# Delta rule with both directions in one tile's halves, its state steps between inversion levels

## The reference

```python
def chunk_gated_delta_rule(q, k, v, beta, g, s0):      # chunks of C = 64
    G = jnp.cumsum(g, axis=-1)
    decay = jnp.exp(jnp.where(incl, G[..., :, None] - G[..., None, :], -jnp.inf))
    kb = k * beta[..., None]
    a = jnp.where(strict, jnp.einsum('nbhid,nbhjd->nbhij', kb, k) * decay, 0.0)
    m = a + jnp.eye(C, dtype=a.dtype)
    rhs = jnp.concatenate([kb * jnp.exp(G)[..., None], v * beta[..., None]], axis=-1)
    sol = lax.linalg.triangular_solve(m, rhs, left_side=True, lower=True, unit_diagonal=True)
    w, u = sol[..., :dk], sol[..., dk:]
    ...
    def step(s, xs):                                   # the state step, one chunk after another
        v_new = u_c - jnp.einsum('bhcd,bhde->bhce', w_c, s)
        o = jnp.einsum('bhcd,bhde->bhce', qd_c, s) + jnp.einsum('bhij,bhje->bhie', qk_c, v_new)
        s = s * cd_c[..., None, None] + jnp.einsum('bhcd,bhce->bhde', kt_c, v_new)
        return s, o
```

## Time and profile before

| | |
|---|---|
| median of 3 runs | 1901.72 us (1900.16 to 1902.12) |
| profiled execution, its own time | 1902.44 us |
| its span on the core | 1900.6 us |
| PE busy, share of span | 1583.7 us, 83% |
| DVE / ACT / POOL busy | 670.8 / 445.5 / 203.8 us |
| mean granted TensorE clock | 0.925 of full speed |
| HBM traffic | 303.79 MB read, 24.78 MB written |

### The profile page before, as it was taken

The page is one execution under the profiler, slowest core; times in us unless marked ns, Lnnn a source line. Parts: engine busy times, 40 slices in busy tenths (PEclk is TensorE's granted clock), DMA queues, the critical chain, the costliest instruction groups (busy, mean ns, idle before and its releaser), DMA issues.

```text
span 1900.6 us, 36972 instructions
## 1 busy us (share of the span) xinstructions
PE 1583.7 (83%) x16252; PEld 1046.0 (55%) x16252; DVE 670.8 (35%) x1293; ACT 445.5 (23%) x722; POOL 203.8 (11%) x202
## 2 busy tenths in 40 slices
PE   5999956779749999978999877687766976999993
PEld 2554424445437776654655455576765545777662
DVE  5134575552350000013142398544454143000003
ACT  4111284441121111103010256421211032111110
POOL 0000000000001111100000000344441000111103
PEclk8999996998869999989999898899988987999996
DMA  9822461454229999982212000000001414999994
GB/s 347 284 89 89 165 244 43 153 204 179 87 76 341 375 388 389 381 279 74 89 44 92 0 1 1 2 2 2 2 2 67 167 58 163 377 372 388 382 392 155
DMA packets 90218, 330.01 MB, mean 174 GB/s; under 512 B 10612, under 2 KB 16360, under 8 KB 81928
## 3 DMA queue, kind: packets, MB, share of 16 engines
q1 hardware_dynamic: 75920, 287.29, 39.6%
q0 software_dynamic: 9168, 32.65, 6.2%
q10 hardware_dynamic: 5032, 8.65, 1.3%
HBM read 303.79 MB, written 24.78 MB: 173 GB/s over the span
## 4 chain that ended last, share of the span: by engine, by line
PE 69%; DVE 15%; DMA 5%; issue 5%; ACT 4%; ACTq 0%; DVEq 0%; POOL 0%; SPq 0%
PE pairs L191 25%; PE pairs L1241 13%; PE pairs L1253 11%; DMA ring<-in_exp_w 3%; PE pairs L1224 2%; DVE sm L1576 1%; PE pairs L417 1%; PE pairs L1871 1%; PE pairs L957 1%; PE pairs L1642 1%; PE pairs L1873 1%; ACT arena L1511 1%; PE pairs L1078 1%; PE pairs L567 1%; DMA ring<-in_w_in_ab 1%
## 5 line engine op out<-in xcount | busy, mean ns | idle before, releaser
L191 PE MATMUL pairs<-hT,ring 128*128 128x128 f32 (+1 forms) x1120 | 305.6, 435 | 2.1 <-ACT hT L315 2.1
L191 PEld LDWEIGHTS pairs<-hT,ring 128*128 128x128 f32 x1120 | 170.0, 192 | 138.5 <-issue 137.1
L315 ACT ACTIVATE arena<-pairs 128x256 f32<-128x256 f32 (+7 forms) x188 | 120.5, 655 | 517.0 <-PE pairs L191 254.4
L191 PE MATMUL pairs<-ring,hT 128*128 128x512 f32 (+1 forms) x448 | 177.4, 557 | 0.0
L1241 PEld LDWEIGHTS pairs<-arena 128*64 128x64 f32 x4096 | 145.6, 139 | 13.8 <-issue 13.7
L1241 PEld LDWEIGHTS pairs<-arena,ring 128*64 128x64 f32 x4096 | 142.8, 137 | 14.1 <-issue 14.1
L1241 PE MATMUL pairs<-arena 128*64 128x80 f32 x4096 | 148.5, 235 | 2.0 <-ACT arena L1274 1.0
L1241 PE MATMUL pairs<-arena,ring 128*64 128x80 f32 x4096 | 145.6, 233 | 1.1 <-issue 1.1
L191 PEld LDWEIGHTS pairs<-ring,hT 128*128 128x128 f32 x448 | 84.8, 190 | 92.2 <-issue 89.1
L1307 DVE TENSOR_SCALAR hT<-pairs,arena 80x512 f32<-80x512 f32 x32 | 23.9, 747 | 273.1 <-ACT hT L1283 273.1
L1253 PE MATMUL pairs<-ring,arena 128*80 128x512 f32 x256 | 112.8, 593 | 1.1 <-DMA ring<-in_exp_w 1.1
(11 more groups left out here) (374 smaller groups left out, 2168.3 us busy)
## 6 DMA issues: line engine op xcount, KB each, us to landing
arena<-in_exp_w SPq DMA_DIRECT2D x48, 2048.0 KB, 19.4
ring<-in_exp_w SPq DMA_DIRECT2D x48, 2048.0 KB, 21.5
ring<-in_w_mod SPq DMA_DIRECT2D x24, 2048.0 KB, 8.1
ring<-in_w_in_ab SPq DMA_DIRECT2D x5, 2048.0 KB, 11.5
ring<-in_w_in_cd SPq DMA_DIRECT2D x5, 2048.0 KB, 7.8
ring<-in_w_out SPq DMA_DIRECT2D x4, 2048.0 KB, 8.6
moe_rows<-arena POOLq DMA_DIRECT2D x2, 2560.0 KB, 16.2
h_rows<-arena POOLq DMA_DIRECT2D x2, 2560.0 KB, 8.4
```

The lines of the kernel that those rows point to most:

```text
L191: last = pe.matmul(out, lhs(k), rhs(k), start=(k == 0), stop=(k == KD - 1))
L315: return eng.activation(dst, src, ACT.Copy) if eng is nc.scalar else eng.tensor_copy(dst, src)
```

## The change

**Mixed tiles.** A tile m < 4 now holds forward tokens on partitions 0 to 63 (the first half of token tile m) and backward tokens on partitions 64 to 127 (the second half of token tile 3 - m). A step j = 0 to 7 does chunk j of the forward and chunk 7 - j of the backward direction, both in tile `tile_at(j)`; j = 8, 9 are the prompt. Each tile serves two steps. The transposes of k and q and the products `kk` are made once per tile (5 times, 10 before), and `kk` is kept in SBUF by ACT (`kk_read`); DVE's `kk_gated` reads that copy. Two steps (j, j + 1) are inverted together.

**Placing.** The state steps of j - 2 and j - 1 stand between the levels 1 and 3 of the inversions of j and j + 1 on every engine; `state_a` is vs and q times state, `state_b` the other two products. The steps 8 and 9 come at the end. PSUM is used in 8 single banks. `wu` no longer uses block-diagonal operands (no memsets of them).

**Around it.** `conv_pe` turns a tile's halves by two matmuls against the identity; the gates are copied in halves (`read_gate`), the decays' columns rearranged by 28 small copies on DVE (`decay_dve`), constants loaded by 6 more DMAs on SP, and `cyT` puts the halves back by its identity's columns.

```diff
@@ -1690,48 +1715,91 @@
+        tile_at = lambda j: 4 if j >= 8 else j // 2 if j % 2 == 0 else 3 - j // 2
+        half_of = lambda j, d: d ^ (j % 2)
+        first_visit = lambda j: j < 4 or j == 8
+        STATE_STEPS = (0, 1, 2, 3, 4, 5, 6, 9)
+        KX_STEPS = (0, 1, 2, 3, 4, 5, 6, 8, 9)
+        TILE_ORDER = (0, 3, 1, 2, 4)
...
@@ -1739,9 +1807,14 @@ def conv_pe(pe):
-                for t in range(NT):
-                    o = t * P if t < ST else UP0
-                    last = pe.transpose(ps[:, t * P:t * P + P], c[:, o:o + P], ident)
+                for m in range(NT):
+                    out = ps[:, m * P:m * P + P]
+                    if m < ST:
+                        for h, r in enumerate(HALF):
+                            o = P * (m if h == 0 else 3 - m) + CK * h
+                            last = pe.matmul(out[r], c[:, o:o + CK], ident, start=True, stop=True)
+                    else:
+                        last = pe.transpose(out, c[:, UP0:UP0 + P], ident)
...
@@ delta_pe
+            for m in TILE_ORDER[:2]:
+                kq(m)
+                kk(m)
+            for j in range(2):
+                am(j)
+            for i in range(5):
+                j = 2 * i
                 for s in range(1, 6):
+                    for e in range(2):
+                        level_w(j + e, s)
+                    if s in (1, 3) and i == 0:
+                        kq(TILE_ORDER[2 + s // 2])
+                    elif s in (1, 3):
+                        state_a(j - 2 + s // 2)
+                    elif s in (2, 4) and i < 4:
+                        dec(j + 1 + s // 2)
+                    elif s == 5 and i == 2:
+                        kq(ST)
+                    for e in range(2):
+                        level_x(j + e, s)
+                    if s in (1, 3) and i == 0:
+                        kk(TILE_ORDER[2 + s // 2])
+                    elif s in (1, 3):
+                        state_b(j - 2 + s // 2)
+                    elif s in (2, 4):
+                        qd(j - 1 + s // 2)
+                    elif s == 5 and i == 2:
+                        kk(ST)
+                if i < 4:
+                    for e in range(2):
+                        am(j + 2 + e)
+                for e in range(2):
+                    wu(j + e)
+            state_b(8)
+            state_a(9)
+            state_b(9)
...
@@ delta_dve
+            def kk_gated(j):
+                v.wait_ge(S("dl_exp"), j + 1)
+                b_emptied(v, ("kk", tile_at(j)))
+                step(v.tensor_tensor(decays(j), kk_all(tile_at(j)), decays(j), ALU.mult))
...
+                for s in range(1, 6):
+                    if s in (1, 3) and i:
+                        values_new(j - 2 + s // 2)
+                    elif s in (2, 4) and i < 4:
+                        dec_read(v, step, j + 1 + s // 2)
+                    for e in range(2):
+                        x_next(j + e, s)
+                    if s in (1, 3):
+                        if i:
+                            state_new(j - 2 + s // 2)
+                        if i < 4:
+                            diag(v, j + 2 + s // 2)
+                    elif s in (4, 5) and i < 4:
+                        kk_gated(j + s - 2)
+                    if i >= 3:
+                        k = 2 * (i - 3)
+                        if s == 1 and i == 4:
+                            o_sum(v, 7, dscr3, 0)
+                        elif s == 2 and i == 4:
+                            o_scale(1)
+                        elif s == 3:
+                            o_sum(v, 6 + k, dscr3, 0)
+                        elif s == 4:
+                            o_scale(k)
...
@@ delta_act
+            def uw_read(j):
+                if j >= 2:
+                    b_filled(act, ("o", 7) if j == 9 else ("st", j - 2, half_of(j, 1)))
+                for b in range(2):
+                    u = ("wu", j, b)
+                    b_release(copy(act, uw(j)[:, 512 * b:512 * b + 512], b_filled(act, u)), u)
...
+                    if s in (3, 5) and i < 4:
+                        decay_exp(act, j + 2 + s // 5)
...
```

More of the change, by code:

```diff
@@ L42, with __init__ @@
 LAM_INIT = 0.2
-WHOLE = ("ident", "ones", "lo_one", "up_one", "block")
-BLOCKS = ["ident", "lo_neg", "up_neg"] + [f"{d}{s}" for d in "fb" for s in range(6)]
+WHOLE = ("ident", "ones", "cum0", "cum1", "block")
+BLOCKS = ["ident", "neg0", "neg1"] + [f"level{e}{s}" for e in range(2) for s in range(6)]
 class Units:
-    def __init__(self):
-        self.uses = [0] * 4
+    def __init__(self, n=4):
+        self.uses = [0] * n
         self.of = {}
@@ new lines, in build, with b_take, b_finish, b_filled @@
+        bank_free = [S(f"bank_free{i}") for i in range(8)]
+        bank_of = lambda b: PSUM[:, b // 2, 512 * (b % 2):512 * (b % 2) + 512]
+        def b_take(pe, name, b):
+            b, n = banks.add(name, b)
+            if n > 1:
+                pe.wait_ge(bank_free[b], n - 1)
+            return bank_of(b)
+        def b_finish(ins, name):
+            ins.then_inc(bank_full[banks.of[name][0]], 1)
+        def b_filled(eng, name):
+            b, n = banks.of[name]
+            eng.wait_ge(bank_full[b], n)
+            return bank_of(b)
@@ new lines, in dec, with qd, am @@
+            def dec(j):
+                pe.wait_ge(S("dl_diag"), j + 1)
+                u = ("dec", j)
+                b_finish(dec_sums(pe, b_take(pe, u, 6), j), u)
+            def qd(j):
+                pe.wait_ge(S("dl_qd"), j + 1)
+                u = ("qd", j)
+                ps = b_take(pe, u, 7)
+                for h in range(4):
+                    last = pe.transpose(ps[:, h * P:h * P + P], qe(j)[:, h, :], ident)
+                b_finish(last, u)
+            def am(j):
+                pe.wait_ge(S(f"dl_am{j % 2}"), 6 * (j // 2) + 1)
+                u = ("am", j)
+                ps = b_take(pe, u, j % 2)
+                for h in range(4):
+                    for r in HALF:
+                        last = pe.matmul(ps[r, CK * h:CK * h + CK], am64(j)[r, h, :], C64["ident"][r, :],
+                                         start=True, stop=True)
+                b_finish(last, u)
@@ L1930, in delta_pe @@
+            state_b(8)
+            state_a(9)
+            state_b(9)
             pe.wait_ge(S("o_done"), 10)
+            for b in range(8):
+                pe.wait_ge(bank_free[b], banks.uses[b])
             for b in range(4):
@@ L1933, in delta_pe @@
                 ps = take(pe, u)
-                for t in range(NT):
-                    last = pe.transpose(ps[:, t * P:t * P + P], oacc[:, t, b * P:b * P + P], ident)
+                for m in range(NT):
+                    out = ps[:, m * P:m * P + P]
+                    if m < ST:
+                        o, gap = ((0, 448), (128, 192), (192, 64), (64, 320))[m]
+                        out = ps[:, o:o + 2 * gap].rearrange("p (a x) -> p a x", a=2)[:, :, 0:CK]
+                    last = pe.transpose(out, oacc[:, m, b * P:b * P + P], swap if m in (2, 3) else ident)
                 finish(last, u)
@@ L1939, in build, with decay_exp @@
         heads5 = lambda x: x.rearrange("p (t h) d -> p t h d", h=4)
[L1941 to L1944 removed]
+        def decay_exp(act, j):
+            (emptied if j < 2 else b_emptied)(act, ("dec", j))
+            act.activation(decays(j), decays(j), ACT.Exp).then_inc(S("dl_exp"), 1)
         def decay_act(act):
@@ L2049, in delta_dve @@
                 conv_read(v, ct)
+            for c in range(2):
+                step(v.tensor_copy(swap[:, CK * c:CK * c + CK], ident[:, CK - CK * c:P - CK * c]))
             for j, x in enumerate((qsq, ksq)):
@@ L2057, in delta_dve @@
             step(v.tensor_scalar(ssq[:, 0:20], ssq[:, 0:20], P ** -0.5, None, ALU.mult))
-            for d in range(2):
-                step(v.memset(slot(d, XT_), 0.0))
             def unit_rows(tiles):
```

774 lines of the change are left out of this document (396 added, 378 removed).

## The result

The changed kernel takes 1860.14 us (median of 4 runs, 1859.9 to 1863.33) against 1901.92 (4 runs, 1900.16 to 1905.5) before: ratio 0.9783, 95% interval 0.9768 to 0.9799, a gain of 42 us. The forecast was 1856.0 in 1836 to 1880, with 0.95 for faster. Its profiled execution has a span of 1861.5 us and a mean clock of 0.922 (before 1900.6 and 0.925).

The account below looks back on a forecast made before the run. The loop was taken as bound by a PE, DVE, PE chain in the state steps and by PE in the levels. 252.7 - 200.7 - 6.0 = 46.0 us off 1902.44 gave 1856.4, stated as 1856, range 1836 to 1880.

Parts of the forecast that it names:

- The pairs: Loop's five pairs of steps i = 0 to 4, then steps 8 and 9 alone: PE work plus waits, 200.7 us together.
- dec stands behind two w products ... 0.95 late, twice a pair: Between levels, PE's dec waits for diag, queued on DVE behind two state updates: 1.9 us a pair, 3.4 from step 4.
- The second am: At a pair's end PE waits for ACT's copies and exponential, DVE's kk_gated at 1.41 and POOL's mask: 2.2 us.
- wu of the second tile needs both banks ... 1.4: At a pair's end the second wu waits until ACT has read both banks of the first: 1.4 us.
- Sum 32.5: PE's work at full clock for a pair with two state steps between its levels: 32.5 us.
- Together 5.8: All PE waits that the new order makes in a middle pair: 5.8 us, so the pair costs 38.3.
- The clock rival: PE falls to 1.2 GHz and stays there; half the loop's work at that level gives 1934 us; chance 0.04.
- Conversion and entry: Ahead of the loop: conv_pe's blocks cost 2.8 us more, two tiles' kq and kk 3.2 more; together 6.0.
- The drain: Changing the tiling mode drains PE's array; at 0.3 us each, 40 changes add up to 12 us, to 1868.
- PE alone: Rival: everything counted as a wait is hidden and PE's work alone bounds the loop: 1827 us; chance 0.09.
- The queues couple: Rival: slower POOL operations and scalings beside DVE and hand-offs in the levels gain 26 us less: 1882; chance 0.12.
- No overlap, 1898: Rival: state steps stay exposed, only kq and kk save 10 us against 6 ahead: 1898; chance 0.02.

Follow-up runs that it names:

- e8: Changed kernel with diag ahead of the state update, separate banks for the second wu, the second exponential and kk_gated earlier, output scaling later: 1829.6 us.
- e9: e8 with each pair's state steps behind wu, none between the levels, and so without the diag edit: 1849.3 us.
- e12: e8 with unused transposes of the identity added where PE waits ahead of the loop: 1825.5 us.
- e1: Changed kernel with each pair's two state steps put back behind its wu, in a row, none between the levels: 1869.1 us.
- e3: Changed kernel with the second tile's wu writing banks of its own: 1853.2 us.
- e11: e1 with kq's transposes and kk's products each issued twice: 1874.9 us.

## Why the prediction was right, and where it was not

The total is 4 us off, and the profiled execution 6.9 above its 1856.4: 4.6 in the loop (205.3 for "Sum 200.7"), 0.7 ahead of it (6.7 for "Together 6.0", the first w standing at 1215.07 where it stood at 1208.4) and 1.7 behind it, which the sum had at nothing. Step by step:

- **The pairs.** Predicted 32.2, 38.3, 40.0, 43.3, 31.8 and 15.1 for the end; measured, from one pair's first w to the next pair's, 35.7, 40.9, 39.2, 43.8, 30.7 and 15.0.
- **"dec stands behind two w products ... 0.95 late, twice a pair".** Measured 0.68 and 1.41, together 2.1 for 1.9. They differ because the second diag took 1.15 us beside POOL and the first, which POOL's overlapped for its last 0.26 us, 0.42. From step 4 on 1.75 and 1.37, 3.1 for 3.4.
- **The second am, "2.2 of wait".** Measured 1.75. "I take 1.41, since POOL is busy there" was wrong: kk_gated took 0.73 and 0.69. Where it runs POOL is idle but for 0.2 us, because POOL's masks wait for it; the lower of the two prices was right. The rule of the Trainium skill (GPSIMD Engine Reference, Specifications) on VectorE's SBUF interface did show, but on the second diag, an operation on two SBUF operands that I had priced without it.
- **"wu of the second tile needs both banks ... 1.4".** Measured 1.36, and 1.30 in i = 0. That wu has "as many column passes" holds only nearly: at full clock the two together took 4.19 us in e8 and e9, for 3.84.
- **The clock**, the step that failed most. "The drop came behind waits of 3 us, and I count none over 2 but in i = 3": the drops came behind 1.75 and 1.36 too. In i = 1 wu took 3.03 + 3.87 instead of 2.13 + 2.13, and w and vs behind it also ran low. The pair missed by 2.6, and that is a sum of errors: PE's work at full clock is 31.2 (e8) for "Sum 32.5", the idle time 5.5 for "Together 5.8", and the lower clock, for which the sum had nothing, added 4.2. i = 3 came within 0.5 of its 43.3 by luck: PE busy for 35.2 and idle for 8.6, where 32.5 and 10.8 were forecast. In i = 2 the prompt's kq and kk keep am's wait at 0.94, wu takes 2.13 + 2.13, and the pair came out 0.8 below its forecast. The clock rival as priced, a lasting 1.2 GHz, did not occur; the loop's clock is 0.90, on the edge that I named.
- **i = 0** missed by 3.5: its first 4.93 us read a clock of 0.50, which the sum had at full, and its pair reads 0.88. In e12, where the entry ran at full clock, i = 0 took 30.0 us, with waits at its end that are 2.1 shorter.
- **Conversion and entry.** 2.2 between the first block and kq for the 2.8, 13.9 for 13.4 from kq to w; the other 0.8 stands ahead of the first block. The 2.2 is not the 2.8 confirmed: a block cost 1.28 at full clock (1183.24 to 1184.52) for "1.1", and the last block was followed by 6.30 of idle that DVE ended. SP's added DMAs cost nothing: the weights' matmuls start at 78.67, not later than 80.04.
- **The drain** of the Trainium skill (TensorEngine Tiling (Array Packing), Key Properties), up to 12 us in the range: no stretch shows it. In the rows of i = 1 above, kv in one mode follows qk in another after 1.02 us, and w follows kv after 1.10, each what their 16 records last or less. A drain of the 0.3 priced would also lift e8's pair above the forecast of its work, and it lies below.
- **The rivals.** "PE alone" needed the waits hidden; e8 shows what it looks like, 33 us a pair, and that it takes four more edits. (By its own sum it is 1826, not 1827, with the 0.7 that the forecast takes off.) "The queues couple": behind the entry, no w waits for POOL at all. "No overlap, 1898": here the working was wrong though the case did not arise. I priced the kernel without overlap as the old one less kq and kk. e1 has no overlap and takes 1869, since DVE's share of the chain PE, DVE, PE had also become shorter.

So the total was right, partly by errors that cancel, and the account of where it comes from was not. The sum set new pairs against old steps; it never asked what a serial state step costs in the new program. Had it counted DVE's operations between the last product and the next vs, two instead of four, it would have credited 1.4 of the 2.98 us to that, the 0.88 ahead of qk to the subtraction in one operation, and the 1.27 ahead of the first vs to the second tile's wu standing there. In place of the state steps hidden between the levels, the runs show: placing 9, DVE's fewer operations 13 to 16, shared products 4 to 6, and 13 to 15 of the rest of the mixed tiles, which no run takes apart.

## What to carry to other kernels

Before crediting a gain to overlap, price the serial order in the new layout: here two half-height DVE operations cost twice one of full height, and taking operations off the path was worth 13 to 16 us, where hiding the chain was worth 9, and 15 to 20 once the other waits were gone. When PE is the bound, repair all the waits at one place together: here each edit alone left PE another wait, and the profiled loop lost 17 us by the four added up and 32 by the four together. Where a wait on PE cannot be removed, fill it with matmuls that nobody reads, and look at the granted clock behind it, in every pair and not in one.

## What the runs showed of the hardware

- The clock fell behind waits under 2 us, but not by their length alone. In e3 the one wait left at the end of i = 1, 1.75 us, was followed by wu at 6.86 us for 4.19, while in e8 one of 2.07 at the same place was followed by 4.19 and a clock of 1.00. In e12 the same 2.07 at the same place was followed by am at 1.98 for 1.15 and four times 1.97 in wu. What else decides was not settled.
- Work added at the lower clock can cost nothing: e11's doubled kq of the second tile took the same 1.94 us as the single one in the changed kernel. It was the first tile's doubled work, 1.7 us each for kq and kk, that paid for it.
- A DVE operation of 128x256 on two SBUF operands took 0.42 us with POOL idle (L2233 at 1279.07) and 1.15 beside it (L2173 at 1273.08); two state updates, with one operand in PSUM, took 1.29 us (L2272 at 1271.88) while POOL worked from 1271.91 on, no more than the 1.28 elsewhere.
